# Expert rows fetched by index against all expert tiles streamed through the matrix engine

## The chip, the cores and the metric

The kernel runs on one core of a Trainium2 chip. The engines of a core are TensorE (PE in the profile, its weight loads PEld), VectorE (DVE), ScalarE (ACT), GpSimd (POOL) and SyncE (SP, which only issues transfers here). The metric is the device time of one execution in microseconds (us), lower is better. The program is one launch, all in float32.

## The reference

A first block of two layers (convolution, attention, cross-attention, layer norm) is followed by a second one: attention and a gated recurrence, merged and added to x, then an expert layer, then a gated projection of side inputs. The change touches the expert layer, cut here to its core:

```python
def peer_ffn(h, w_q, sub_keys, u, v):          # T = 512 tokens, D = 1024, 8 heads, K = 16 picks a head
    q = (ht @ w_q).reshape(T, PEER_HEADS, 2, PEER_DKEY // 2)
    s = jnp.einsum('thpc,hpnc->thpn', q, sub_keys)
    v1, i1 = lax.top_k(s[:, :, 0], K)
    v2, i2 = lax.top_k(s[:, :, 1], K)
    cand = (v1[..., :, None] + v2[..., None, :]).reshape(T, PEER_HEADS, K * K)
    cand_idx = (i1[..., :, None] * PEER_NKEYS + i2[..., None, :]).reshape(T, PEER_HEADS, K * K)
    top_s, pos = lax.top_k(cand, K)
    idx = jnp.take_along_axis(cand_idx, pos, axis=-1)
    g = jax.nn.softmax(top_s, axis=-1)
    # per block of 128 tokens:
    ue = jnp.take(u, ib, axis=0)               # u, v: 16384 x 1024, float32, 64 MiB each
    w = jax.nn.gelu(jnp.einsum('thkd,td->thk', ue, xb)) * gb
    out = jnp.einsum('thk,thkd->td', w, jnp.take(v, ib, axis=0))
```

Each token so needs 128 of the 16384 rows of u and as many of v.

## The kernel before

Tokens lie 128 to a block, four blocks. Everything up to the merged sum of the second block is a chain of matrix products over 2 MB weight slots, which SP streams into two buffers W (L505) as PE gives them back (`used`, L547); the change leaves it alone. Around position 1700 us of the span the part begins that is changed:

- PE runs `xT_f(0)`, `xT_f(1)` (transposes of the normed rows of blocks 0 and 1), `queries` for one of the four slots of w_q, `merge(2)` and `merge(3)` (the last products of blocks 2 and 3, L988), and then the remaining queries. `queries` is `project_fm` (L537, 32 products of 128x256 or 128x512) and then the products with the sub-keys (L1034); ACT copies the results out (L1490, L1137) and counts up `sk_ready`.
- DVE selects the picks, one head of one block at a time (`route_step`, L2116 to L2153): the 16 best of two lists of 128 scores, the 256 sums of these pairs, the 16 best sums, and the two ranks turned back into key numbers by comparing with 0 to 15 (L2144 to L2147).
- As soon as a head has its picks, POOL issues one indexed transfer for each of its 16 picks (`gather_u`, L1567): 128 rows of u, one for each token, 512 KB, into a ring of 8. DVE multiplies and sums each against h (L2246), ACT and DVE make gelu and softmax of 16 numbers a token, and POOL fetches the same picks' rows of v (L1583). ACT writes a diagonal matrix of the 128 weights (L1446) and PE multiplies it with the rows of v, two products of 128x512 (L1017), summed in a bank for each block and half. There are 512 transfers of u and 512 of v; 10 of the last ones are added by DVE.
- Each block that is complete runs its last step (`ple_*`, L1079 to L1106, L2211) beside the picks of the others; the last block's is the end of the program.

The order on each engine is fixed in the program; nothing is scheduled at run time but by semaphores.

## Time and profile before

| | us |
|---|---|
| median of 3 runs (3283.68 to 3296.66) | 3289.33 |
| span of the profiled execution, first to last instruction | 3278.9 |
| PE busy / DVE / ACT / POOL in it | 2812.3 / 1829.2 / 652.2 / 1273.9 |
| read from HBM | 662.19 MB |

The profile is of one execution; its page gives the span and no separate time, so the span stands for it, and the timed median lies 10.4 us above it. "x n" counts instructions; each float32 product shows as two records, a transpose as one. The granted clock of PE is given as a share of its full level of 2.4 GHz.

### The profile page before, as it was taken

How to read it: one execution, taken by the hardware profiler on the slowest of the kernel's cores; microseconds unless marked ns; L12 is line 12 of the kernel's file. 1: busy time of each engine (PE TensorE's matmuls, PEld its weight loads, DVE VectorE, ACT ScalarE, POOL GpSimd, SP SyncE). 2: the span in 40 equal slices, each digit the busy share in tenths (PEclk: the TensorE clock that was granted, in tenths of full speed). 3: DMA queues.
4: the chain of work that ended last, by engine and by line, in shares of the span. 5: the costliest groups of instructions: out<-in, count | busy, mean ns of one | idle time of the engine just before them, and what ended most of it. 6: DMA issues, size and time to landing. Idle time of an engine off the chain costs nothing.

```text
span 3278.9 us, 26326 instructions
## 1 busy us (share of the span) xinstructions
PE 2812.3 (86%) x7932; PEld 1338.4 (41%) x7932; DVE 1829.2 (56%) x4230; ACT 652.2 (20%) x1556; POOL 1273.9 (39%) x1113
## 2 busy tenths in 40 slices
PE   9999999998889899988898889777768786777778
PEld 4455445454554444555555334322223232222323
DVE  4989502058751322267529666576666666666643
ACT  1114301022320112344401111111111111111111
POOL 0520000000000000022104767777777777777774
PEclk9999999999999999999999999999989999999999
DMA  4221122220112111001216999999999999999996
GB/s 179 77 103 52 64 77 77 77 77 26 51 40 77 67 69 51 26 30 49 90 65 216 366 371 368 371 387 373 345 361 371 363 353 367 372 366 352 368 386 244
DMA packets 161469, 665.89 MB, mean 203 GB/s; under 512 B 17856, under 2 KB 18240, under 8 KB 154304
## 3 DMA queue, kind: packets, MB, share of 16 engines
q0 software_dynamic: 147456, 536.94, 43.9%
q1 hardware_dynamic: 12032, 117.43, 9.8%
q10 hardware_dynamic: 1856, 10.00, 0.8%
q8 instruction: 61, 1.00, 0.1%
q14 instruction: 64, 0.52, 0.0%
HBM read 662.19 MB, written 2.10 MB: 203 GB/s over the span
## 4 chain that ended last, share of the span: by engine, by line
PE 54%; POOL 18%; issue 9%; DVE 9%; DMA 7%; ACT 2%; another core or an unknown queue 0%; DVEq 0%; ACTq 0%; POOLq 0%; SPq 0%
PE ps L537 13%; PE ps L1017 8%; POOL G L1567 8%; PE ps L652 6%; POOL H L1583 5%; POOL XT L1583 4%; PE ps L589 4%; PE ps L882 3%; DMA XT<-peer_v,C 3%; DMA H<-peer_v,C 3%; PE ps L790 2%; PE ps L911 2%; PE ps L819 2%; DMA G<-peer_u,C 2%; PE ps L976 2%
## 5 line engine op out<-in xcount | busy, mean ns | idle before, releaser
L2246 DVE CUSTOM_DVE_ANT_0 G<-G,H 128x1024 f32<-128x1024 f32 x512 | 627.7, 1226 | 465.7 <-DMA G<-peer_u,C 396.0
L1017 PE MATMUL ps<-H,MK 128*128 128x512 f32 x1196 | 591.2, 623 | 190.3 <-DMA H<-peer_v,C 124.0
L1567 POOL DMA_INDIRECT G<-peer_u,C x512 | 540.3, 1055 | 302.9 <-issue 151.8
L537 PE MATMUL ps<-XT,W 128*128 128x512 f32 (+1 forms) x1344 | 543.0, 553 | 8.9 <-issue 6.5
L1017 PE MATMUL ps<-XT,MK 128*128 128x512 f32 x812 | 403.1, 629 | 130.6 <-DMA XT<-peer_v,C 80.3
L1017 PEld LDWEIGHTS ps<-H,MK 128*128 128x128 f32 x1196 | 218.6, 195 | 532.3 <-issue 476.0
L1583 POOL DMA_INDIRECT H<-peer_v,C x304 | 350.6, 1153 | 131.3 <-issue 71.8
L537 PEld LDWEIGHTS ps<-XT,W 128*128 128x128 f32 x1344 | 254.1, 190 | 294.2 <-issue 286.2
L1017 PEld LDWEIGHTS ps<-XT,MK 128*128 128x128 f32 x812 | 149.5, 197 | 381.1 <-issue 326.0
L1542 POOL COPY PR<-H 128x256 f32<-128x256 f32 x4 | 1.4, 392 | 781.2 <-DVE H L1871 781.2
L1446 ACT ACTIVATE MK<-C 128x128 f32<-128x128 f32 x502 | 175.0, 393 | 524.5 <-PE ps L1017 292.6
L1583 POOL DMA_INDIRECT XT<-peer_v,C x208 | 241.1, 1159 | 78.7 <-issue 48.5
L652 PE MATMUL ps<-W,Y 128*128 128x512 f32 x512 | 226.1, 603 | 13.1 <-DVE Y L1746 6.1
L589 PE MATMUL ps<-XT,W 128*128 128x512 f32 x448 | 220.5, 604 | 1.6 <-ACT G L1152 1.6
L1554 POOL TENSOR_TENSOR H<-H 128x256 f32<-128x256 f32 x56 | 47.6, 852 | 353.9 <-ACT H L1376 320.6
L1645 DVE SCALAR_TENSOR_TENSOR Y<-H,V,Y x240 | 165.3, 765 | 0.0
L652 PEld LDWEIGHTS ps<-W,Y 128*128 128x128 f32 x512 | 98.3, 193 | 140.3 <-issue 137.1
L1433 ACT ACTIVATE H<-C 128x16 f32<-128x16 f32 x32 | 6.9, 216 | 630.3 <-DVE H L2162 336.8
L1528 POOL TENSOR_TENSOR H<-H,SIG 128x512 f32 x12 | 73.5, 6125 | 111.9 <-ACT SIG L1212 108.9
L1755 DVE SCALAR_TENSOR_TENSOR X<-X,H 128x512 f32<-128x512 f32 x16 | 11.1, 691 | 181.9 <-ACT H L1137 181.9
L589 PEld LDWEIGHTS ps<-XT,W 128*128 128x128 f32 x448 | 80.6, 195 | 59.7 <-issue 55.7
L882 PE MATMUL ps<-W,XT 128*128 128x512 f32 x192 | 98.5, 622 | 0.3 <-issue 0.3
(296 smaller groups left out, 3121.3 us busy)
## 6 DMA issues: line engine op xcount, KB each, us to landing
W<-wstream SPq DMA_DIRECT2D x51, 2048.0 KB
G<-peer_u,C POOLq DMA_INDIRECT x512
H<-peer_v,C POOLq DMA_INDIRECT x304
XT<-peer_v,C POOLq DMA_INDIRECT x208
XT<-xT SPq DMA_DIRECT2D x8, 256.0 KB, 5.3
W<-wstream SPq DMA_DIRECT2D x8, 256.0 KB, 5.8
X<-x SPq DMA_DIRECT2D x1, 2048.0 KB, 19.0
SIG<-rows ACTq DMA_DIRECT2D x4, 512.0 KB, 6.4
```

The lines of the kernel that those rows point to most:

```text
L537: mm = pe.matmul(b[:, 0:rhs[k].shape[-1]], w[:, k, m * P:(m + 1) * P], rhs[k], start=(k == 0), stop=(k == KD - 1))
L589: mm = pe.matmul(FILL_BANK[j % 2][:, :], w[:, k, m * P:(m + 1) * P], XT[:, k, :], start=(k == 0), stop=(k == KD - 1))
L652: mm = pe.matmul(ps[pos % 4][:, :], Y[:, (j * KD + k) * T + b * P:(j * KD + k) * T + (b + 1) * P], w[:, k, :], start=(j == 0 and k == 0), ...
L790: mm = pe.matmul(ps[p0 % 4][:, 0:n], XT[:, k, b * P:(b + 1) * P], w[:, k, 0:n], start=(k == 0), stop=(k == KD - 1))
L882: mm = pe.matmul(ring(pos)[:, :], XT[:, k, b * P:(b + 1) * P], w[:, k, :], start=(k == 0), stop=(k == KD - 1))
L1017: mm = pe.matmul(ps[2 * b + half][:, :], DG[by_tensor(v - 1) % DIAG_RING], VB[at][:, half * T:(half + 1) * T], start=(n == FIRST[b] and k ...
L1446: act.activation(DG[at % DIAG_RING], ident, ACT.Copy, scale=GW[:, v:v + 1]).then_inc(diag_full, 1)
L1528: pool.tensor_tensor(hrow(i * 4 + j, TAPS - 1, T), hrow(i * 4 + j, TAPS - 1, T), SIG[:, j, :], ALU.mult).then_inc(glu_done, 1)
L1567: pool.indirect_dma_start(UB[u % U_RING], None, peer_u, bass.IndirectOffsetOnAxis(ap=IDX[:, u:u + 1], axis=0)).then_inc(u_loaded[u % U_RIN ...
L1583: pool.indirect_dma_start(VB[at], None, peer_v, bass.IndirectOffsetOnAxis(ap=IDX[:, v:v + 1], axis=0)).then_inc(v_loaded[at], 16)
L1645: ins = dve.scalar_tensor_tensor(yt(c), hrow(c, k, T), V[:, ds(c * TAPS + (FM["conv_w"] + k), 1)], yt(c), ALU.mult, ALU.add)
L2246: dve.tensor_tensor_reduce(out=rows_u, in0=rows_u, in1=tm(H, 0, D, group(n)[0]), scale=1.0, scalar=0.0, op0=ALU.mult, op1=ALU.add, accum_o ...
```

## The change

The expert layer no longer fetches rows by index. All 128 tiles of 128 experts are streamed in order, u and v of a tile side by side in 1 MB, and every expert is computed for every token; a gate that is zero for an expert that was not picked takes the rest out. The sums for 256 tokens take four of the eight PSUM banks, so the whole is done twice: blocks 0 and 1 in steps 0 to 127, blocks 2 and 3 in steps 128 to 255.

- A step on PE: `expert_dots` (8 products of 128x256, tile of u as weights), then `expert_sums` of the step before (4 products of 128x512, the gated activations as weights, tile of v moving). ACT takes gelu of the 128x256, DVE multiplies with the gates (`weigh`).
- The gates: the picks (two key numbers and the softmax weight, 128 a token) are transposed; for each token one matrix 128x128 with a one in each column's first key, one with the weight at the second key, and their product is that token's 128x128 table of gates. For blocks 0 and 1 this stands ahead of step 0 (64 groups of 4 tokens), for blocks 2 and 3 it lies in steps 37 to 127 (128 pairs of tokens), and DVE selects their picks in steps 0 to 80.
- The queries are computed for blocks 0 and 1 first and for 2 and 3 later, so w_q is loaded twice. The norm ahead of them moves to ACT in part, with its gain put in when the transposes are copied out.
- Selection handles two heads at once (`route`, 35 instructions and more for each of 16 units); the softmax is made over a whole block.
- Buffers are placed by hand over one another (ARENA). The scores of blocks 2 and 3 wait in DRAM.
- POOL has no work left in this part. The last step of blocks 0 and 1 lies in steps 212 to 243, that of 2 and 3 behind step 255.

```diff
-GROUPS = NB * PEER_HEADS
-PICKS = GROUPS * PEER_K
-U_RING = 8
-V_RING = 8
-DIAG_RING = 8
-V_BEHIND = 24
-V_EARLY = 96
-V_LATE = PICKS - 30
-DIAG_AHEAD = 6
-A_RING = 8
-GELU_C = float(np.sqrt(2 / np.pi))
+TILES = 128
+ARENA = 217504
+STEPS = 2 * TILES
+UV_RING = 3
+WA_RING = 4
+PICKED_2, PICKED_3 = 33, 82
...
-                ("gate_c", 4), ("up", 2), ("wq", 4), ("ple", 2)])
+                ("gate_c", 4), ("up", 2), ("wq", 8), ("ple", 2)])
...
+            sp.wait_ge(bank_full, POS["wq3b"] + 6)
+            for m in range(STEPS + 1):
+                if m == UV_RING:
+                    sp.wait_ge(a_full, 1)
+                elif m > UV_RING:
+                    sp.wait_ge(w_used, m - UV_RING)
+                sp.dma_start(UV[:, m % UV_RING, :], experts[m % TILES]).then_inc(uv_loaded[m % UV_RING], 16)
...
-            def expert_row(v):
...
+            for q in range(4):
+                queries(f"wq{q}a", q, (0, 1))
             merge(2)
             merge(3)
...
             xT_f(3)
+            for q in range(4):
+                queries(f"wq{q}b", q, (2, 3))
+
+            def expert_dots(g):
+
+                at = g % UV_RING
+                u = UV[:, at, 0:D].rearrange("p (k e) -> p k e", k=KD)
+                pe.wait_ge(uv_loaded[at], 16 * (g // UV_RING + 1))
+                if g >= 2:
+                    pe.wait_ge(gelu_done, g - 1)
+                c0 = (g // TILES) * 256
+                for k in range(KD):
+                    mm = pe.matmul(UP_BANK[g % 2][:, 0:256], u[:, k, :], XT[:, k, c0:c0 + 256],
+                                   start=(k == 0), stop=(k == KD - 1))
...
+            def expert_sums(g):
+
+                at, j = (g + 1) % UV_RING, g % TILES
+                pe.wait_ge(w_ready, g + 1)
...
+                        mm = pe.matmul(acc(b, n)[:, :], WA[:, g % WA_RING, b * P:(b + 1) * P],
+                                       UV[:, at, D + n * T:D + (n + 1) * T], start=(j == 0), stop=(j == TILES - 1),
+                                       skip_group_check=True)
...
+            def build_pair(p):
+
+                pe.wait_ge(pair_hot, 2 * p + 2)
+                pe.wait_ge(pair_one, p + 1)
+                if p >= 2:
+                    pe.wait_ge(gates_kept, p - 1)
+                for i in range(2):
+                    mm = pe.matmul(BUILD_BANK[p % 2][:, i * P:(i + 1) * P], OHB[:, (2 * p + i) % 6, :], OHB[:, 6 + (2 * p + i) % 6, :],
+                                   start=True, stop=True)
+                mm.then_inc(built, 1)
...
+            pe.wait_ge(tail_free, made)
+            expert_dots(0)
+            for b in range(2):
+                bank(POS["it"] + b)
+                picks_transposed(ring(POS["it"] + b), b).then_inc(bank_full, 1)
+            for n in range(64):
+                pos = POS["build"] + n
+                bank(pos)
+                pe.wait_ge(hot, 4 * n + 4)
+                pe.wait_ge(ones_made if n < 32 else ones_b, n % 32 + 1)
+                for i in range(4):
+                    one = GATES_0[:, 128 + 4 * n + i, :] if n < 32 else ONES_KEPT[:, n % 4, i, :]
+                    mm = pe.matmul(ring(pos)[:, i * P:(i + 1) * P], OHB[:, (4 * n + i) % 12, :], one, start=True, stop=True)
+                mm.then_inc(bank_full, 1)
...
+            for g in range(STEPS):
+                if g + 1 < STEPS:
+                    expert_dots(g + 1)
+                for b in (2, 3):
+                    if g == (PICKED_2, PICKED_3)[b - 2] + 1:
+                        if b == 3:
+                            pe.wait_ge(gates_kept, pairs_by(g - 1))
+                        picks_transposed(MISC_BANK, b).then_inc(it_full, 1)
+                        pe.wait_ge(it_copied, b - 1)
+                for p in pairs_of(g):
...
+                expert_sums(g)
+            ple_transposes(2)
+            ple_transposes(3)
+            for b in (2, 3):
+                ple_gates(b, 0)
+                ple_gates(b, 1)
+                ple_proj(b)
...
+            def gelu(g):
+
+                act.wait_ge(a_full, g + 1)
+                if g >= WA_RING:
+                    act.wait_ge(w_used, g - WA_RING + 1)
+                act.activation(WA[:, g % WA_RING, :], UP_BANK[g % 2][:, 0:256], ACT.Gelu_apprx_tanh).then_inc(gelu_done, 1)
+
+            def pair_ones(p):
+
+                if p % 64 == 0:
+                    act.wait_ge(it_copied, p // 64 + 1)
+                if p >= 3:
+                    act.wait_ge(built, p - 2)
+                at = 6 + (2 * p) % 6
+                for i in range(2):
+                    n = ac.count(act.activation(OHB[:, at + i, :], IOTA, ACT.Abs, scale=-1.0,
+                                                bias=IT[:, 0, 2 * p + i:2 * p + i + 1]))
+                ac.after(n)
+                act.activation(OHB[:, at:at + 2, :], OHB[:, at:at + 2, :], ACT.Relu, scale=-1.0, bias=1.0
+                               ).then_inc(pair_one, 1)
+
+            def keep_pair(p):
+
+                act.wait_ge(built, p + 1)
+                act.wait_ge(w_ready, p + 1)
+                act.activation(GATES_1[:, :, :, p], BUILD_BANK[p % 2][:, 0:256].rearrange("p (q i) -> p q i", q=2), ACT.Copy
...
+            exponentials(0)
+            drain(POS["it"], lambda bk: act.activation(
+                IT[:, :, 0:P], bk[:, 0:3 * P].rearrange("p (i t) -> p i t", i=3), ACT.Copy))
+            act.wait_ge(bank_free, POS["it"] + 1 + 4)
+            act.wait_ge(scores_out, 32)
+            for n in range(32):
+                for i in range(4):
+                    last = ac.count(act.activation(GATES_0[:, 128 + 4 * n + i, :], IOTA, ACT.Abs, scale=-1.0,
+                                                   bias=IT[:, 0, 4 * n + i:4 * n + i + 1]))
+                ac.after(last)
+                act.activation(GATES_0[:, 128 + 4 * n:132 + 4 * n, :], GATES_0[:, 128 + 4 * n:132 + 4 * n, :], ACT.Relu,
+                               scale=-1.0, bias=1.0).then_inc(ones_made, 1)
+            exponentials(1)
+            drain(POS["it"] + 1, lambda bk: act.activation(
+                IT[:, :, P:2 * P], bk[:, 0:3 * P].rearrange("p (i t) -> p i t", i=3), ACT.Copy))
+            gelu(0)
+            for n in range(64):
+                drain(POS["build"] + n, copy_to(GD[:, n * T:(n + 1) * T]))
+            act.wait_ge(bank_free, POS["end"] + 4)
+            act.dma_start(KEPT[:, :], kept[0]).then_inc(scores_back, 16)
...
+            for g in range(STEPS):
+                for b in (2, 3):
+                    if g == (PICKED_2, PICKED_3)[b - 2] + 1:
+                        picks_copied(b)
+                for p in pairs_of(g + 1):
+                    pair_ones(p)
+                if g + 1 < STEPS:
+                    gelu(g + 1)
+                for p in pairs_of(g):
+                    keep_pair(p)
...
-            def gather_u(u):
...
-            def gather_v(v):
...
+            drawn(route(0, 0))
+            drawn(route(0, 1))
+            unit = route(0, 2)
+            drawn(unit, 16)
+            residual_sum(2)
+            drawn(unit)
+            row_factor(2)
+            residual_sum(3)
+            unit = route(0, 3)
+            drawn(unit, 16)
+            row_factor(3)
+            drawn(unit)
+            soft_start(0)
+            unit = route(1, 0)
+            drawn(unit, 12)
+            soft_end(0)
+            drawn(unit)
+            for q in range(1, 4):
+                drawn(route(1, q))
+            soft_start(1)
+            soft_end(1)
+
+            def hot_row(at, t, done):
+                dve.tensor_scalar(OHB[:, at, :], IOTA, IT[:, 1, t:t + 1], IT[:, 2, t:t + 1], ALU.is_equal, ALU.mult
+                                  ).then_inc(done, 1)
+
+            rows4 = [P, 4, P]
...
+            for n in range(64):
+                if n % 32 == 0:
+                    dve.wait_ge(bank_free, POS["it"] + n // 32 + 1 + 4)
+                if n >= 3:
+                    dve.wait_ge(bank_full, POS["build"] + n - 2)
+                for i in range(4):
+                    hot_row((4 * n + i) % 12, 4 * n + i, hot)
+                if n >= 32:
+                    if n >= 36:
+                        dve.wait_ge(bank_full, POS["build"] + n - 3)
+                    dve.tensor_tensor(ONES_KEPT[:, n % 4, :, :],
+                                      IOTA.rearrange("p (t i) -> p t i", t=1).broadcast_to(rows4),
+                                      IT[:, 0, 4 * n:4 * n + 4].rearrange("p (t i) -> p t i", i=1).broadcast_to(rows4),
+                                      ALU.is_equal).then_inc(ones_b, 1)
+
+            def weigh(g):
+
+                if g == 0:
+                    dve.wait_ge(bank_free, POS["end"] + 4)
+                if g == TILES:
+                    dve.wait_ge(gates_kept, TILES)
+                dve.wait_ge(gelu_done, g + 1)
+                w = WA[:, g % WA_RING, :]
+                if g < TILES:
+                    dve.tensor_tensor(w, w, GATES_0[:, :, g], ALU.mult).then_inc(w_ready, 1)
+                else:
+                    w = w.rearrange("p (j q) -> p q j", q=2)
+                    dve.tensor_tensor(w, w, GATES_1[:, :, g - TILES, :], ALU.mult).then_inc(w_ready, 1)
+
+            def hot_pair(p):
...
+            for g in range(STEPS):
+                weigh(g)
+                for p in pairs_of(g + 1):
+                    hot_pair(p)
+                if g < PICKED_3 - 1:
+                    i, quota = route_quota(g)
+                    drawn_of[i] += drawn(routes[i], quota - drawn_of[i])
...
```

ACT, from the last queries to the first work for the experts. Before (EXPS and the diagonals stand behind the third of the half queries):

```order
L1426 ACTIVATE XT<-ps 128x4x128 [waits bank_full] x3
L1490 ACTIVATE SIG<-ps 128x256 [waits bank_full] x4
L1137 ACTIVATE Y<-ps 128x512 [waits bank_full] x2
L1433 ACT_TABLE_LOAD [waits bank_free]
L1433 ACTIVATE H<-C 128x16 [waits tanh_in]
L1434 ACTIVATE H<-H 128x16
L1446 ACTIVATE MK<-C 128x128 [waits weights]
L1446 ACTIVATE MK<-C 128x128 x6
```

And now, behind the eighth query (EXB holds the exponents of the softmax, IT the transposed picks, GD the gates):

```order
L1513 ACTIVATE SIG<-ps 128x256 [waits bank_full] x3
L1195 ACTIVATE Y<-ps 128x512 [waits bank_full] x2
L1522 ACT_TABLE_LOAD [waits bank_free]
L1522 ACTIVATE EXB<-EXB 128x128 [waits soft_in]
L1601 ACTIVATE IT<-ps 128x3x128 [waits bank_full]
L1607 ACTIVATE GD<-C,IT 128x128 [waits scores_out,bank_free]
L1607 ACTIVATE GD<-C,IT 128x128 x3
```

The first exponential now stands behind all query copies of all four blocks, and the one-hot rows L1607 behind it.

DVE at the same place of the changed program (L2268 starts the softmax of block 0, L2272 ends it, L2212 to L2221 are the selection of block 1, L2309 the rows that hold the weights); there is no softmax of a block before, but a head's:

```order
L2268 TENSOR_TENSOR EXB<-BG 128x128 [waits dve_link]
L2212 MAX TOPV<-KEPT 128x8 [waits sk_ready]
L2212 MAX TOPV<-KEPT 128x8 x3
L2216 MAX_INDEX TOPI<-TOPV,KEPT 128x8 [waits dve_link] x4
L2221 MATCH_REPLACE KEPT<-TOPV,KEPT 128x128 [waits dve_link] x4
L2272 TENSOR_REDUCE SMX<-EXB 128x8 [waits soft_exp]
L2273 RECIPROCAL SMX<-SMX 128x8 [waits dve_link]
L2274 TENSOR_TENSOR BG<-EXB,SMX 128x128 [waits dve_link]
L2212 MAX TOPV<-KEPT 128x8 [waits dve_link]
```

```order
L2259 TENSOR_REDUCE PK<-HOT 128x2x32 [waits dve_link]
L2268 TENSOR_TENSOR EXB<-BG 128x128 [waits dve_link]
L2272 TENSOR_REDUCE SMX<-EXB 128x8 [waits soft_exp]
L2273 RECIPROCAL SMX<-SMX 128x8 [waits dve_link]
L2274 TENSOR_TENSOR BG<-EXB,SMX 128x128 [waits dve_link]
L2309 TENSOR_SCALAR OHB<-C,IT 128x128 [waits bank_free]
L2309 TENSOR_SCALAR OHB<-C,IT 128x128 x11
L2309 TENSOR_SCALAR OHB<-C,IT 128x128 [waits bank_full]
```

The wait for `soft_exp` stands in the middle of the selection of block 1, and the first L2309 behind the whole of it.

PE in the stage of the experts, before (a diagonal as weights, rows of v moving):

```order
L1017 MATMUL ps<-XT,MK 128x512 [waits v_loaded4,diag_full]
L1017 MATMUL ps<-XT,MK 128x512
L1017 MATMUL ps<-XT,MK 128x512 [waits v_loaded5,diag_full]
L1017 MATMUL ps<-XT,MK 128x512
...
L1017 MATMUL ps<-H,MK 128x512 [waits v_loaded0,diag_full]
L1017 MATMUL ps<-H,MK 128x512
```

And a step with a pair of tokens now:

```order
L1072 MATMUL ps<-UV,WA 128x512 [waits w_ready]
L1072 MATMUL ps<-UV,WA 128x512 x3
L1056 MATMUL ps<-XT,UV 128x256 [waits gelu_done,uv_loaded2]
L1056 MATMUL ps<-XT,UV 128x256 x7
L1095 MATMUL ps<-OHB 128x128 [waits pair_one,pair_hot]
L1095 MATMUL ps<-OHB 128x128
L1072 MATMUL ps<-UV,WA 128x512 [waits w_ready]
L1072 MATMUL ps<-UV,WA 128x512 x3
```

Waits for a fetched row and a diagonal at each pair of products become one wait for the tile and one for the gated activations in a step of 12 products.

## Rows read from the trace of the kernel before

**Rows 1.** The page: chain of waits by engine, DVE's dots, PE's diagonal products.
```profile
PE 54%; POOL 18%; issue 9%; DVE 9%; DMA 7%; ACT 2%; another core or an unknown queue 0%; DVEq 0%; ACTq 0%; POOLq 0%; SPq 0%
L2246 DVE CUSTOM_DVE_ANT_0 G<-G,H 128x1024 f32<-128x1024 f32 x512 | 627.7, 1226 | 465.7 <-DMA G<-peer_u,C 396.0
```

**Rows 2.** Windows: us, busy of PE, PEld, DVE, ACT, POOL, clock, DMA, GB/s.
```profile
1200.00:1300.00 100.00, 99.45 (x306) 46.35 (x305) 15.56 (x46) 23.13 (x47) 0.00 (x0) 1.00 0.18 66
1789.00:3279.00 1490.00, 1135.06 (x2472) 450.83 (x2472) 934.29 (x2368) 225.53 (x664) 1102.14 (x999) 0.96 0.96 360
```

**Rows 3.** Timeline of PE: start, us, instructions, idle before.
```profile
1702.12 1.94 PE L575 MATMUL ps<-C,H 128*128 128x128 f32 x16 [0.26 <-issue]
1719.47 2.05 PE L1034 MATMUL ps<-MK,SIG 128*128 128x128 f32 x16 [0.47 <-ACT SIG L1490]
1721.36 1.04 PE L575 MATMUL ps<-C,MK 128*128 128x128 f32 x8
...
1730.38 7.03 PE L988 MATMUL ps<-H,XT 128*128 128x512 f32 x16
1737.25 1.04 PE L575 MATMUL ps<-C,MK 128*128 128x128 f32 x8
...
1772.28 14.05 PE L537 MATMUL ps<-XT,W 128*128 128x256 f32 x64 [1.17 <-issue]
...
1789.12 0.67 PE L537 MATMUL ps<-XT,W 128*128 128x256 f32 x2 [0.26 <-issue]
1801.08 3.66 PE L1017 MATMUL ps<-H,MK 128*128 128x512 f32 x4 [11.29 <-DMA H<-peer_v,C]
...
1805.01 1.88 PE L1017 MATMUL ps<-H,MK 128*128 128x512 f32 x4
```

**Rows 4.** Timeline of ACT in the same stretch.
```profile
1712.13 0.38 ACT L1490 ACTIVATE SIG<-ps 128x256 f32<-128x256 f32 x1 [3.07 <-PE ps L537]
1715.58 0.38 ACT L1490 ACTIVATE SIG<-ps 128x256 f32<-128x256 f32 x1 [3.07 <-PE ps L537]
...
1788.00 0.60 ACT L1137 ACTIVATE Y<-ps 128x512 f32<-128x512 f32 x1 [1.25 <-PE ps L1034]
1789.60 1.28 ACT L1433 ACT_TABLE_LOAD   x1
...
1794.08 2.15 ACT L1446 ACTIVATE MK<-C 128x128 f32<-128x128 f32 x7 [2.77 <-DVE C L2171]
```

**Rows 5.** Timeline of DVE: two heads selected one after the other, then block 2's sum.
```profile
1722.24 0.62 DVE L2116 MAX8 H<-Y 128x8 f32<-128x128 f32 x2 [18.86 <-ACTq L1494]
...
1733.17 0.62 DVE L2116 MAX8 H<-Y 128x8 f32<-128x128 f32 x2
...
1744.28 1.29 DVE L2075 TENSOR_TENSOR X<-X,ps 128x512 f32<-128x512 f32 x2
```

**Rows 6.** Groups of DVE by form, from 1600 us: busy, mean ns.
```profile
L2144 DVE TENSOR_TENSOR H<-H,C 128x256 f32<-128x256 f32 x64 | 26.9, 421 | 0.1
...
L2138 DVE TENSOR_SCALAR H<-H 128x16 uint32<-128x16 uint32 x32 | 5.5, 171 | 0.1
...
L2193 DVE TENSOR_SCALAR Y<-ps,V 128x128 f32<-128x128 f32 x16 | 4.5, 345 | 0.9 <-PE ps L1079 0.8
```

**Rows 7.** DMA issues: KB each, median us to landing.
```profile
X<-x SPq DMA_DIRECT2D x1, 2048.0 KB, 19.0
...
Y<-wstream ACTq DMA_DIRECT2D x1, 2048.0 KB, 8.1
...
MK<-subkeys ACTq DMA_DIRECT2D x1, 1024.0 KB, 5.6
```

**Rows 8.** Timeline of all engines at the end.
```profile
3253.76 3.67 PE L1017 MATMUL ps<-XT,MK 128*128 128x512 f32 x8 [1.08 <-DMA XT<-peer_v,C]
...
3260.26 13.97 PE L1091 MATMUL ps<-W,Y 128*128 128x512 f32 x32 [0.72 <-ACT Y L1455]
```

736 lines of the change are left out of this document (360 added, 376 removed), and 5 rows, old and new, of the table at.

## The prediction

> **What bounds the kernel now.** I read the chain of waits first, then the groups of instructions, then windows and timelines. The chain names PE for 54%, then POOL, DVE and DMA in pieces [rows 1]: up to 1700 us the program is a row of matrix products, and the last 1490 us are something else. In the first part PE is busy 99% of a window at a granted clock of 1.00 [rows 2]. In the stage of the experts PE is busy 1135 of 1490 us, while the transfers hold 0.96 of the DMA engines at 360 GB/s, and DVE's dots wait 396 us for rows of u [rows 1, 2]. So this stage is set by the bytes it fetches: 1024 transfers of 512 KB are 537 MB, and at 360 GB/s that is 1491 us. It starts near 1789 and ends with the span. This is what the change can take away, and it replaces it by 2 x 128 tiles of 1 MB = 268 MB, half the bytes, and by far more products.
>
> **What a step costs on PE.** The price of float32 products stands in the trace twice. With 256 columns: ACT copies out a bank each time 8 of them are done, and two copies start 3.45 us apart [rows 4]; that is 0.431 us a product. With 512 columns: 16 records (8 products) from 1730.38 to the next group at 1737.25 are 6.87 us, 0.859 a product [rows 3]. A step has 8 of the first and 4 of the second: 3.45 + 3.44 = 6.89 us. 256 steps are 1764; the first dots stand ahead of the loop, so 1760. Nothing can hide this, PE is the engine that works, and it alone is longer than the stage that it replaces (1490).
>
> Also on PE in the loop: the 128 pairs of the second half, 256 products of 128 columns at 0.236 (16 records from 1719.47 to 1721.36 [rows 3]) = 60 us; the last step of blocks 0 and 1, 40 products of 512 columns = 34, and 16 transposes at 0.12 [rows 3] = 2; twice a wait until ACT has copied the transposed picks, 2 each = 4. Loop: 1760 + 60 + 36 + 4 = 1860. The waits at tile and gated activations cost nothing if they are met early: products of two kinds with waits between them follow at full pace from 1805 on [rows 3]. If each step lost 0.1 at a wait it would be 26 more.
>
> Here a rule of the Trainium skill speaks against the change, and the rows first: in the window 1200 to 1300 PE is busy 99.45 us and the weight loads 46.35 us more, 146 us in 100, so loads run beside products [rows 2], with 256 columns too, where 64 records take 14.05 us [rows 3]. The page "TensorE: Matmul & The Clock Gate" of the Trainium skill, section "Part 3: Packing small matmuls — row/col tiling", says that a weight load overlaps products in flight only when it goes to another row group. Every product here uses all rows, so by the rule each of 24 loads a step would add to it; that is rival four below.
>
> **Ahead of the loop.** Positions in the span:
> - Transposes of blocks 0 and 1 start at 1702.1 as before. Their copies now carry the gain in pieces of 128x128, 16 at the 0.29 of ACT's seven in a row (2.15 less one's 0.39, by 6 [rows 4]) = 4.7: queries from 1707.
> - A query of two blocks is 16.84, from 1772.28 to 1789.12 [rows 3]. Four stand ahead of the merges now: 1774.5. The second load of w_q is hidden, a 2 MB slot landed in 8.1 [rows 7] and a query takes twice that; SP's queue then holds the scores' way out (2 MB) ahead of the first tiles, which have until 1955.
> - Two merges, 15.9 each (1721.36 to 1737.25 [rows 3]): 1806.3. They come 53 us later than before, and block 3's sum on DVE, which sits in the middle of block 0's selection, waits for them. Then the sum 0.65 (half of 1.29 for two [rows 5]), square and root on ACT 1.4, 16 selection instructions 5.5 (a quarter of the 22.04 for two heads [rows 5]), scaling 1.2 (DVE's 1024 elements are 1.23 [rows 1]), transposes and copies 2.5, 11 us: queries of blocks 2 and 3 from 1817, and again 67.4: 1884.5.
> - ACT's first exponential stands behind the last of these copies: table load 1.28 [rows 4] and itself, 1886. DVE has finished block 0 and 12 instructions of block 1 at about 1830 and waits 56 us for it, with the rest of block 1's selection queued behind.
> - One `route` (two heads): before, two heads one after the other are 22.04 us [rows 5]. Of that, 12 instructions of 256 elements become 3 of 1024 (0.42 against 1.23 [rows 1, 6], each with 0.03 to the next: 12 x 0.45 against 3 x 1.26): -1.7; the 14 short ones of 0.17 [rows 6] and their gaps become 5: -2; fewer links and one sum of 512 instead of two: -0.9. 17.4. DVE still owes 13 of the started one and three more: 1886 + 13 + 52 = 1951, softmax, transposes and copy 4: 1955. ACT's one-hot rows run beside it (32 x about 1.9 = 61 from 1894, when the scores are out in DRAM): also 1955. If these rows take 0.39 each without overlap it is 1970.
> - The 64 groups of the first half: PE needs 4 x 0.236 = 0.95, ACT a copy of 0.60 [rows 4]; DVE 4 rows of 128x128 with two scalars, which the trace doesn't show. Bounds: 0.17 (16 elements) and 0.345 (128 from PSUM, [rows 6]); I take 0.26. 32 groups at 1.05, and 32 at 1.7, since the comparison for 4 tokens (128x512, half of the 1.29 for two [rows 5]) joins: 88 us, with bounds of 74 and 110. Loop starts at 1955 + 88 + 2 = 2045.
>
> On these rows the Trainium skill's page "VectorE: DVE Perf Modes", section "What auto-detection actually checks", says that an operation with one source in SBUF takes two float32 elements a cycle. By its 0.96 GHz a row would be 0.07 shorter than one from PSUM; an estimate by that page makes the groups some 6 us shorter than I take them. No row here shows this size.
>
> **Behind it.** From the last products (3253.76 + 3.67) to the end of the span are 21.5 us with one block's gate products of 13.97 in it [rows 8]. Now two blocks stand there and the side products are not done earlier: 21.5 + 13.7 + 2 x 3.4 = 42.
>
> Sum: 2045 + 1860 + 42 = 3947 against a span of 3278.9; with the 10.4 around it 3957.
>
> **What lies beside.** DVE in a step: 0.42 for the gates, in steps 0 to 31 four to five selection instructions (70 us in 32 steps, 2.2 each), later 1.5 and up to four rows at 0.26: under 4 of 6.89. The gates are read 512 bytes apart; from 0.42 (packed, [rows 6]) to four times that it stays hidden, because gelu and gates have a whole step to be ready: `expert_sums` of step g waits behind the sums of g-1 and the dots of g+1. ACT: 0.4 for gelu, two pairs at 1.5: 3.4. Transfers: 1 MB took 5.6 us and 2 MB 8.1 [rows 7]; each has 13.8 us from the buffer's release to its use and two are under way.
>
> **The rivals.**
> 1. Gates or gelu late: a row of long selection instructions (three of 1.26) or a slow strided read passes 6.89 - 0.4 - 0.4 = 6 us in a step, from there each us counts. For: all three engines meet at every step. Against: 4 us as worked out. 1 us in each of the first 128 steps: 3957 + 128 = 4085.
> 2. The stream is late: the slowest 2 MB took 19.0 [rows 7], 9.5 a tile, 2.6 over the step: 256 x 2.6 = 670, 4627. That one was issued among other transfers at the start; the stage now moves 360 GB/s and needs 152.
> 3. Not slower: the stage goes at the pace of its bytes, as it does now. 268 MB at 360 GB/s are 746 us, and 2045 + 746 + 42 + 10 = 2843. It decides below (3279 - 2045 - 42 - 100) / 256 = 4.27 us a step. For: DMA is what this stage waits for today. Against: the products of a step are priced by rows at full clock, 6.89; they would have to be 38% cheaper than anywhere in this trace.
> 4. Weight loads not hidden: 46.35 / 305 = 0.15 each [rows 2], 24 a step: 3.6 x 256 = 930, 4890. The same window contradicts it. It is the skill's rule above; the trace disagrees with it.
> 5. The clock. After 11.29 us of waiting four records took 3.66 instead of 1.88 [rows 3], the lower of the two levels. That is paid once or twice ahead of the loop (PE waits from 1890 to 1955), 2 to 5 us; in the loop PE has no waits that would bring it. Inside the forecast's range.
>
> **Chances.** The forecast 0.86, its own range 3910 to 4040 (groups -14 to +22, ACT's rows to +15, waits in the loop 0 to +26, slips ahead of the loop +20). Rival 1 0.06, rival 2 0.03, rival 3 0.03, rival 4 0.01; 0.01 that the result is level for a cause that I don't see. A measurement of this kernel can tell about 0.5% from no change. So slower 0.96, same 0.01, faster 0.03. The range, 3900 to 4070, leaves out the top of rival 1 and all others.
>
> **What would show it.** Step: 256 dots groups 6.9 us apart where no pair lies between, 7.4 to 7.8 with pairs, PE over 98% busy at clock 1.00 from 2045 on. DVE idle some 56 us ahead of L2272 once, and the loop's first L1072 at 2045 to 2050. HBM read about 400 MB, DMA near 0.4 in the loop. Wrong if PE waits for `w_ready` or the tiles over 50 us in sum, if products of 256 columns are not half those of 512, or if the groups of the first half take over 110 us.

## The result, and the profile after

The changed kernel takes 3945.72 us (median of 4 runs, 3944.23 to 3946.36); the kernel before took 3286.51 beside it (3272.77 to 3296.66). The ratio is 1.2018 [1.1991, 1.2044]: 20% slower, against 3957 us forecast.

The page of the changed kernel: span, busy time, the chain of waits by engine, groups of instructions, the tiles' transfers.

```profile
span 3942.3 us, 35590 instructions
PE 3727.5 (95%) x13232; PEld 2284.9 (58%) x13232; DVE 1357.3 (34%) x3436; ACT 876.1 (22%) x2011; POOL 142.7 (4%) x89
...
HBM read 404.83 MB, written 4.19 MB: 104 GB/s over the span
...
PE 88%; DVE 7%; ACT 3%; issue 2%; DMA 0%; DVEq 0%; POOL 0%; ACTq 0%; SPq 0%; POOLq 0%
...
L1056 PE MATMUL ps<-XT,UV 128*128 128x256 f32 x4096 | 928.0, 380 | 11.0 <-DMA UV<-experts 10.8
L1072 PE MATMUL ps<-UV,WA 128*128 128x512 f32 x2048 | 920.8, 592 | 0.6 <-ACT IT L1555 0.6
...
L2340 DVE TENSOR_TENSOR WA<-WA,GD 128x256 f32<-128x256 f32 x128 | 54.6, 426 | 850.3 <-ACT WA L1529 850.3
...
L2337 DVE TENSOR_TENSOR WA<-WA,GD 128x256 f32<-128x256 f32 x128 | 77.6, 606 | 625.3 <-ACT WA L1529 623.4
...
UV<-experts SPq DMA_DIRECT2D x257, 1024.0 KB, 4.8
```

PE's share of the chain went from 54% to 88%. POOL (18% before [rows 1]) and DMA (7%) are gone from it, and DVE went from 9% to 7%. The bytes fell from 662 to 405 MB. PE waited for a tile once (10.8 us, at the first dots, ahead of the loop). For the gated activations it never waited: the 0.6 us at L1072 is a wait for ACT's copy of the transposed picks. DVE and ACT do the waiting now. The multiplication with the gates took 0.606 us where 256 gates lie 512 bytes apart (blocks 0 and 1), and 0.426 where they lie packed in two runs of 128, with the activations read and written at a step of two words (blocks 2 and 3).

Windows of the changed kernel (columns as in [rows 2]), ahead of the loop and inside it:

```profile
1885.00:1960.00 75.00, 7.80 (x26) 6.23 (x27) 54.60 (x212) 59.32 (x164) 0.00 (x0) 0.55 0.19 69
1960.00:2050.00 90.00, 74.02 (x529) 66.42 (x528) 83.72 (x281) 39.76 (x67) 0.00 (x0) 0.98 0.03 12
2050.00:2300.00 250.00, 249.42 (x870) 164.85 (x869) 81.80 (x287) 19.07 (x46) 0.00 (x0) 1.00 0.46 156
3000.00:3500.00 500.00, 500.00 (x1747) 331.65 (x1746) 30.67 (x72) 27.65 (x72) 0.00 (x0) 1.00 0.48 165
```

From 3000 to 3500 PE is busy for every one of 500 us at clock 1.00, while the transfers hold 0.48 of the DMA engines. The stage of [rows 2], which moved 360 GB/s at a share of 0.96, has become one that moves 165 at the pace of its products.

The timeline of PE in the changed kernel (columns as in [rows 3]): the start of the queries for blocks 2 and 3, their end, the hole ahead of the gates, the start of the loop, a step with a pair, the end.

```profile
1813.45 15.87 PE L534 MATMUL ps<-XT,W 128*128 128x256 f32 x64 [2.21 <-issue]
...
1878.82 2.05 PE L1015 MATMUL ps<-MK,SIG 128*128 128x128 f32 x16 [0.47 <-ACT SIG L1513]
1891.65 5.67 PE L1056 MATMUL ps<-XT,UV 128*128 128x256 f32 x16 [10.78 <-DMA UV<-experts]
1897.15 0.38 PE L1085 MATMUL ps<-C,PK 128*128 128x128 f32 x2
...
1958.08 0.66 PE L1085 MATMUL ps<-C,PK 128*128 128x128 f32 x2 [60.44 <-DVE BG L2274]
...
1959.07 11.16 PE L1149 MATMUL ps<-GD,OHB 128*128 128x128 f32 x75
...
2045.31 3.62 PE L1056 MATMUL ps<-XT,UV 128*128 128x256 f32 x16
2048.77 3.60 PE L1072 MATMUL ps<-UV,WA 128*128 128x512 f32 x8
2052.20 3.62 PE L1056 MATMUL ps<-XT,UV 128*128 128x256 f32 x16
...
2679.74 0.61 PE L1095 MATMUL ps<-OHB 128*128 128x128 f32 x4
2680.18 3.60 PE L1072 MATMUL ps<-UV,WA 128*128 128x512 f32 x8
2683.62 3.62 PE L1056 MATMUL ps<-XT,UV 128*128 128x256 f32 x16
2687.07 0.61 PE L1095 MATMUL ps<-OHB 128*128 128x128 f32 x4
...
3894.09 7.03 PE L1072 MATMUL ps<-UV,WA 128*128 128x512 f32 x16
...
3903.74 13.97 PE L1122 MATMUL ps<-GD 128*128 128x512 f32 x32 [0.39 <-issue]
```

A step is 2052.20 - 2045.31 = 6.89 us, with a pair 2687.07 - 2679.74 = 7.33. The loop goes from 2045.31 to 3901.12: 1855.8. The tail behind it is 41.2. So the 663 us that the span grew by (3942.3 - 3278.9) have three parts: the loop starts 256 us behind 1789, near which the stage of the experts started before; it is 366 us longer than the 1490 us of that stage; and the tail, which lay inside the 1490, is another 41.

DVE and then ACT in the changed kernel, the same stretch: three holes of the one, one of the other ahead of the gates.

```profile
1883.25 0.29 DVE L2272 TENSOR_REDUCE SMX<-EXB 128x8 f32<-128x128 f32 x1 [61.66 <-ACT EXB L1522]
...
1898.28 0.75 DVE L2212 MAX8 BG<-CAND 128x8 f32<-128x256 f32 x2 [11.39 <-ACT IT L1601]
...
1957.08 0.29 DVE L2272 TENSOR_REDUCE SMX<-EXB 128x8 f32<-128x128 f32 x1 [7.36 <-ACT EXB L1522]
```

```profile
1897.68 0.49 ACT L1601 ACTIVATE IT<-ps 128x384 f32<-128x384 f32 x1 [14.46 <-PE ps L1085]
1898.21 1.28 ACT L1607 ACTIVATE GD<-C,IT 128x128 f32<-128x128 f32 x4
1899.52 0.63 ACT L1610 ACTIVATE GD<-GD 128x512 f32<-128x512 f32 x1
1900.05 1.26 ACT L1607 ACTIVATE GD<-C,IT 128x128 f32<-128x128 f32 x4
```

DVE's first hole is the wait for the exponential behind the queries' copies, as forecast. The second was not forecast: block 1's best sums go into BG, which holds block 0's weights until they are transposed, and those transposes stand on PE behind the first dots, which wait for tile 0. ACT waits for the same transposes, 14.5 us, and then makes its 32 groups of one-hot rows, one each 1.83 us, 58.6 in sum: 1898.2 to 1956.8. Block 1's exponential stands behind them; that is DVE's third hole. So of the two chains that lead to the gates, one over DVE's selection and one over ACT's one-hot rows, ACT's ended last.

### The profile page after: what moved, and what is told of

Read it like the earlier page. It is cut to its first block, busy times and chain, and to the rows that moved or that the text cites. A ratio compares the mean times of both kernels' runs of the same rounds, so it can differ in the third digit from the quotient of the medians.

```text
span 3942.3 us, 35590 instructions
## 1 busy us (share of the span) xinstructions
PE 3727.5 (95%) x13232; PEld 2284.9 (58%) x13232; DVE 1357.3 (34%) x3436; ACT 876.1 (22%) x2011; POOL 142.7 (4%) x89
## 4 chain that ended last, share of the span: by engine, by line
PE 88%; DVE 7%; ACT 3%; issue 2%; DMA 0%; DVEq 0%; POOL 0%; ACTq 0%; SPq 0%; POOLq 0%
PE ps L1056 22%; PE ps L1072 22%; PE ps L534 13%; PE ps L649 5%; PE ps L586 3%; PE ps L879 2%; PE ps L787 2%; PE ps L908 2%; PE ps L816 2%; DVE OHB L2309 2%; PE ps L1095 1%; PE ps L985 1%; PE ps L973 1%; PE ps L1122 1%; ACT GD L1607 1%
## 5 line engine op out<-in xcount | busy, mean ns | idle before, releaser
L1056 PE MATMUL ps<-XT,UV 128*128 128x256 f32 x4096 | 928.0, 380 | 11.0 <-DMA UV<-experts 10.8
L1072 PE MATMUL ps<-UV,WA 128*128 128x512 f32 x2048 | 920.8, 592 | 0.6 <-ACT IT L1555 0.6
L1056 PEld LDWEIGHTS ps<-XT,UV 128*128 128x128 f32 x4096 | 779.4, 190 | 226.2 <-issue 133.0
L1072 PEld LDWEIGHTS ps<-UV,WA 128*128 128x128 f32 x2048 | 382.0, 190 | 379.6 <-issue 370.7
L1529 ACT ACTIVATE WA<-ps 128x256 f32<-128x256 f32 x256 | 98.2, 384 | 1485.9 <-PE ps L1056 1485.9
L2340 DVE TENSOR_TENSOR WA<-WA,GD 128x256 f32<-128x256 f32 x128 | 54.6, 426 | 850.3 <-ACT WA L1529 850.3
L2337 DVE TENSOR_TENSOR WA<-WA,GD 128x256 f32<-128x256 f32 x128 | 77.6, 606 | 625.3 <-ACT WA L1529 623.4
L2309 DVE TENSOR_SCALAR OHB<-C,IT 128x128 f32<-128x128 f32 x512 | 142.5, 342 | 32.3 <-PE ps L1095 31.2
L1539 ACT ACTIVATE OHB<-C,IT 128x128 f32<-128x128 f32 x256 | 84.8, 381 | 29.1 <-PE ps L1095 29.1
L1765 DVE SCALAR_TENSOR_TENSOR Y<-H,V,Y 128x512 f32<-128x512 f32 x120 | 81.1, 745 | 0.0
L1095 PEld LDWEIGHTS ps<-OHB 128*128 128x128 f32 x512 | 71.2, 191 | 5.4 <-ACT IT L1555 0.8
```

The costliest lines, as they stand in the source:

```text
L1056: mm = pe.matmul(UP_BANK[g % 2][:, 0:256], u[:, k, :], XT[:, k, c0:c0 + 256], start=(k == 0), stop=(k == KD - 1))
L1072: mm = pe.matmul(acc(b, n)[:, :], WA[:, g % WA_RING, b * P:(b + 1) * P], UV[:, at, D + n * T:D + (n + 1) * T], start=(j == 0), stop=(j == ...
L1095: mm = pe.matmul(BUILD_BANK[p % 2][:, i * P:(i + 1) * P], OHB[:, (2 * p + i) % 6, :], OHB[:, 6 + (2 * p + i) % 6, :], start=True, stop=True)
L1529: act.activation(WA[:, g % WA_RING, :], UP_BANK[g % 2][:, 0:256], ACT.Gelu_apprx_tanh).then_inc(gelu_done, 1)
L1539: n = ac.count(act.activation(OHB[:, at + i, :], IOTA, ACT.Abs, scale=-1.0, bias=IT[:, 0, 2 * p + i:2 * p + i + 1]))
L2309: dve.tensor_scalar(OHB[:, at, :], IOTA, IT[:, 1, t:t + 1], IT[:, 2, t:t + 1], ALU.is_equal, ALU.mult).then_inc(done, 1)
```

## The experiments

The experiments ran on three chips: the first four on one, the next four on a second and the last three on a third. The kernel before was timed beside each group: 3283.14, 3292.22 and 3227.46 us. A ratio is always to the time of its own group; times and spans of kernels whose loop is set by PE are compared with the changed kernel's directly (two edits that should change nothing, below, came within 1.4 us of it).

The theory: the time is PE's float32 products, 6.89 us a step, and nothing else in the loop counts; ahead of the loop a chain over DVE and ACT sets the start. The rivals: the step is set by the tiles' transfers, by ACT and DVE between dots and sums, or by a fixed cost of each step.

**Half of the sums.** In the steps in between, the sums for the second 512 columns are left out.

```
+                        if n == 1 and 0 < j < TILES - 1:
+                            continue
                         mm = pe.matmul(acc(b, n)[:, :], ...
```

> Leaves out the second 512 output columns of the weighted sums in tiles 1 to 126 of both passes: 504 of the 1024 products of 128x512; everything else, the 1 MB a step too, stays. Theory (the loop runs at PE's price of the columns, 0.859 us a product): 504 x 0.859 = 433 us less, 3946 -> 3513. Rival (the stream sets the step): no change, 3946. Rival (gelu and gates arrive just in time, the step is their chain): under 100 us less, with PE waiting for w_ready.

3514.83 us (3514.51 to 3517.16), ratio 1.0697 [1.0665, 1.0729], span 3513.0: 429.3 us less than the changed kernel's span. Left out are 2 x 126 steps of two products: 252 x 2 x 0.859 = 433. So nearly every us of products taken out is a us of time.

**Half of the dots too.** Four of the eight dots (k 2 to 5) left out as well.

```
+                    if 1 < k < 6:
+                        continue
```

> As half_sums, and 4 of the 8 dots of each step left out too: 1024 products of 128x256 at 0.431 are another 441 us. Theory: a step of 3.45 us, 3946 - 433 - 441 = 3072, since the stream then needs 305 GB/s and the engines beside PE at most 4 us in some steps (selection, up to 30 us late in sum): 3070 to 3110. Rival stream: if 1 MB can't come faster than every 4.8 us (its time to landing), 256 x 4.8 = 1229 for the loop, 3300. Rival chain: 3500 or more.

3085.83 us (3084.72 to 3086.63), ratio 0.9389 [0.9361, 0.9417], span 3083.8. Again 429 less (255 x 4 x 0.431 = 440 are left out). A step is down to 2 x 1.72 = 3.44 us, half of 6.89, below the 4.27 at which the third rival was to decide, and the kernel is faster than before. The transfers still keep up: where no pairs lie between the steps they move 305 GB/s, and PE is busy all the time.

```profile
2600.00:2700.00 100.00, 100.00 (x350) 66.25 (x349) 12.37 (x29) 11.14 (x29) 0.00 (x0) 1.00 0.85 305
```

**A fifth of a step.** Two dots and one product of the sums.

```
+                    if 0 < k < 7:
+                        continue
...
+                        if b + n > 0 and 0 < j < TILES - 1:
+                            continue
```

> Leaves out 6 of 8 dots a step, and 3 of 4 weighted sums in tiles 1 to 126: PE needs 1.72 us a step. Theory: PE alone would give 2635; the next bound is the stream, 268 MB at the 360 GB/s that the gathers reached, 2.9 us a step, so 2850 to 3000, with PE waiting for tiles by then. If a tile can't follow before 2 x its time to landing in a ring of three (4.8 / 2 = 2.4 a step) that is hidden behind it. A rival in which DVE or ACT bound the first 128 steps (selection, rows, gates, 3 to 4 us a step): 3000 to 3150, with PE's waits on w_ready.

2934.33 us (2922.96 to 2939.84), ratio 0.8919 [0.8884, 0.8955]. Only 148 us less in the span (2935.4), though about as many us of products are gone again. Two windows of this run, a piece of the loop and the whole loop:

```profile
2500.00:2700.00 200.00, 136.49 (x368) 74.36 (x367) 26.00 (x61) 23.43 (x61) 0.00 (x0) 0.89 0.94 351
2043.00:2894.00 851.00, 637.19 (x2170) 374.19 (x2168) 320.74 (x993) 305.36 (x802) 0.00 (x0) 0.94 0.87 323
```

In the first window PE is busy 136 of 200 us and the transfers hold 0.94 at 351 GB/s: now the tiles set the pace, and PE waits 195 us for them in the loop. The time is 91 us over the third rival's 2843, the floor of the bytes. The second window shows where they are: over the whole loop the stream makes 323 GB/s at a share of 0.87, and the loop takes 851 us, where 746 were worked out from 360 GB/s (105 more; the loop's start, the tail and the times around the span give 11 back in this execution, which took 2937.34). PE waits only 14 us for gated activations, so DVE's work accounts for little of it.

**The upper halves.** The lower 16 bits of each operand of dots and sums are not used: a float32 word's upper half, read with a step of two, is the number as bf16. Count, columns and order of the products stay.

```
+def high(a, n):
+    return a.bitcast(BF16).rearrange("p (n two) -> p n two", two=2)[:, 0:n, 1]
...
-  mm = pe.matmul(UP_BANK[g % 2][:, 0:256], u[:, k, :], XT[:, k, c0:c0 + 256],
+  mm = pe.matmul(UP_BANK[g % 2][:, 0:256], high(u[:, k, :], P), high(XT[:, k, c0:c0 + 256], 256),
...
-  mm = pe.matmul(acc(b, n)[:, :], WA[...], UV[...], ...
+  mm = pe.matmul(acc(b, n)[:, :], high(WA[...], P), high(UV[...], T), ...
```

> No product is left out, but the dots and the weighted sums read only the upper 16 bits of each float32 word (as bfloat16, every second 16-bit element): same bytes streamed, same instructions, one pass for each product instead of four. Theory (PE's price is four passes a column at 0.42 ns): 8 x 0.11 + 4 x 0.215 = 1.74 us a step, as in fifth_step, so the same time as fifth_step within 2%, 2850 to 3150. Rival (the price is the read of 4-byte elements or of the weights, not the passes): weight loads at 0.19 are 24 or 12 a step and PE stays at 3.5 to 6.9, 3070 to 3946. Operands are cut to 8 bits of mantissa, the picks are not.

2911.11 us (2902.85 to 2916.77), ratio 0.8861 [0.8827, 0.8895]. PE's timeline and the window in this run:

```profile
2131.44 1.08 PE L1063 MATMUL ps<-XT,UV 128*128 128x256 bf16 x8 [2.25 <-DMA UV<-experts]
2132.36 1.06 PE L1079 MATMUL ps<-UV,WA 128*128 128x512 bf16 x4
2133.85 1.08 PE L1063 MATMUL ps<-XT,UV 128*128 128x256 bf16 x8 [0.42 <-DMA UV<-experts]
```

```profile
2500.00:2700.00 200.00, 139.43 (x771) 74.41 (x772) 27.27 (x64) 24.58 (x64) 0.00 (x0) 0.91 0.95 364
```

Eight dots are 0.92 us instead of 3.45 (2131.44 to 2132.36). With every product in its place, only cheaper, the same change is a gain: what costs is the price of float32 products, not their number or the steps' waits. Now PE waits for tiles, which come at 364 GB/s in this window. (The kernel computes with less precise operands; whether that is enough is for its user to judge.)

**The exponential earlier.** Ahead of the loop: ACT takes block 0's exponential behind the first of the late queries' copies.

```
             for q in range(4):
                 queries(f"wq{q}b", q, (2, 3))
+                if q == 0:
+                    exponentials(0)
 
-            exponentials(0)
```

> ACT's first exponential stands behind the first query of blocks 2 and 3 instead of behind the last: soft_exp comes near 1831 instead of 1883. Forecast's picture (DVE waits 54 us for it with block 1's selection behind): the first row of L2309 about 50 us earlier if nothing else is late. Theory after reading the trace: the selection of block 1 is stopped again 3 us later by its write over BG, which waits until PE has transposed block 0's picks; PE does that behind all queries and behind the first dots, which wait for the first tile until 1891.6 (ACT's copy at 1898.2). So 0 to 1 us, 3944 to 3946, and DVE idle ahead of L2212 on BG 60 us instead of 11.

3944.34 us (3943.38 to 3946.23), ratio 1.1974 [1.1941, 1.2006]: nothing. DVE in this run:

```profile
1833.80 0.29 DVE L2273 TENSOR_REDUCE SMX<-EXB 128x8 f32<-128x128 f32 x1 [12.64 <-ACT EXB L1522]
...
1898.14 0.75 DVE L2213 MAX8 BG<-CAND 128x8 f32<-128x256 f32 x2 [60.71 <-ACT IT L1602]
```

The hole of 61.7 us shrank to 12.6, and the second one, 11.4, grew to 60.7. The wait for BG ends at 1898 as before, and with it ACT's wait for the same transposes.

**The transposes ahead of the dots.** Block 0's picks are transposed before the first dots.

```
-            expert_dots(0)
             for b in range(2):
                 bank(POS["it"] + b)
                 picks_transposed(ring(POS["it"] + b), b).then_inc(bank_full, 1)
+                if b == 0:
+                    expert_dots(0)
```

> PE transposes block 0's picks ahead of the first dots instead of behind them. Theory: copy at 1885 instead of 1898; DVE's selection of block 1 goes on 11 us earlier, ACT's one-hot rows start when the scores are out (about 1889), 9 us earlier; the first group of the gates at 1949 instead of 1958: 3946 - 9 = 3937. Rival (the exponential sets this part): no change.

3935.77 us (3935.05 to 3936.52), ratio 1.1947 [1.1914, 1.1979]; span 3933.1, 9.2 less. PE in this run:

```profile
1884.66 0.41 PE L1085 MATMUL ps<-C,PK 128*128 128x128 f32 x2 [3.38 <-DVE BG L2275]
...
1950.33 9.91 PE L1150 MATMUL ps<-GD,OHB 128*128 128x128 f32 x69
```

The gates start at 1950.33 instead of 1959.07. ACT in this run begins its rows so much earlier:

```profile
1889.48 1.28 ACT L1608 ACTIVATE GD<-C,IT 128x128 f32<-128x128 f32 x4 [3.77 <-DMA scores_kept<-Y]
```

That is 8.7 us before 1898.21, and it is now the scores' way out to DRAM that they wait for. So the place of the transposes cost 9 us, by way of ACT's rows.

**More work for DVE in each step of the second half.** Three, and in another kernel six, operations over 1024 elements ahead of the gates.

```
             for g in range(STEPS):
+                if TILES <= g < STEPS - 1:
+                    for _ in range(6):
+                        ch.link(dve.tensor_tensor(HOT[:, :], HOT[:, :], HOT[:, :], ALU.max))
                 weigh(g)
```

> Three operations of 128x1024 on DVE (3.8 us) are put ahead of each step's gates in steps 128 to 254, result unused. Theory: PE sets the step and the gates have 6.88 - 0.38 - 0.43 = 6.0 us of slack: no change, 3946, DVE 4.2 us busy a step. Rival (the chain gelu, gates is what the step waits for, or DVE's reads slow PE's): up to 127 x 3.8 = 480 more.

3944.62 us (3943.96 to 3947.09), ratio 1.1972 [1.194, 1.2005]: nothing, with 3.8 us more on DVE in each of 127 steps.

> Six such operations, 7.6 us with their links, and 0.43 for the gates, so 8.0 a step on DVE alone, over the 6.88 of PE. Theory: above the point DVE sets the step: 127 x (8.0 - 6.9) = 140 more, 4085, and PE waits for w_ready about 1.1 a step. If the point lay lower (no overlap of the chain across steps), it would be 127 x (0.4 + 8.0) = 1070 or more in place of 875, over 4140.

4048.64 us (4048.36 to 4049.72), ratio 1.229 [1.2257, 1.2323]. DVE and PE in this run:

```profile
3303.80 7.52 DVE L2385 TENSOR_TENSOR HOT<-HOT 128x1024 f32<-128x1024 f32 x6
3311.35 0.43 DVE L2340 TENSOR_TENSOR WA<-WA,GD 128x256 f32<-128x256 f32 x1
```

```profile
3303.94 3.70 PE L1072 MATMUL ps<-UV,WA 128*128 128x512 f32 x8 [0.74 <-DVE WA L2340]
...
3311.83 3.70 PE L1072 MATMUL ps<-UV,WA 128*128 128x512 f32 x8 [0.74 <-DVE WA L2340]
```

And its waits (what waits for what: us in total, times, the longest), from 2950 us on:

```profile
PE ps L1072 <- DVE WA L2340: 76.0, 101, 1.8
```

A step is 7.89 us now on both engines, and on DVE it holds nothing but its own work: 3303.45 to 3311.35, six operations and the gates. Gelu does not add to it, since the operations run beside it. So the point of the first rival lies at 6.5 us of other work, not at 6, and past it each us counts (6.89 less the 0.43 of the gates; no run lies between 3.8 and 7.5 us of added work). The sum is +103 us, not 140: PE waits in 101 of the 127 steps, 101 x 1.0 = 101. In the others the 36 us of products of the last steps of blocks 0 and 1 keep PE longer than DVE.

**The whole way to the loop.** Both edits above, with second buffers for the picks of block 1, and the one-hot rows interleaved: ACT makes those of 7 groups ahead and then those of every second group beside the products, DVE the rest (32 groups each, as before, and not the 36 and 28 of the expectation), instead of 32 groups of ACT's ahead of everything. ACT's rows now lie in eight slots, clear of the scores, so its wait for their way out to DRAM moves behind the rows and the first gelu. Dots and sums in float32.

```
+ACT_ONES = list(range(7)) + list(range(7, 56, 2))
+DVE_ONES = [n for n in range(64) if n not in ACT_ONES]
...
+        PKS, BGS = (PK, PK1, PK, PK), (BG, BG1, BG, BG)
...
             for n in range(64):
                 drain(POS["build"] + n, copy_to(GD[:, n * T:(n + 1) * T]))
+                if n + 6 in ACT_ONES[7:]:
+                    ones_of(ACT_ONES.index(n + 6))
```

> The part ahead of the loop without its three waits, products as in the changed kernel: exponential behind the first query of blocks 2 and 3; own copies of picks for block 1, so that its selection need not wait for the transposes; transposes ahead of the first dots; one-hot rows made by ACT and DVE by turns, 36 and 28 groups. Theory: selection of block 1 ends near 1897, first group of the gates near 1900 instead of 1958, the 64 groups 84 to 90 us: loop at 1987 instead of 2045, 3946 - 58 = 3888. Rival (another wait, the first tile or the scores' way out, takes over): 3925 or more.

3886.48 us (3884.15 to 3886.68), ratio 1.2043 [1.1962, 1.2123] against 3227.46 (3210.05 to 3255.02), the time of the kernel before beside these last three. The ratio is no better than the 1.2018 above because the kernel before is 59 us faster here, so the gain is read from the spans. The loop in this run:

```profile
1985.33 3.62 PE L1061 MATMUL ps<-XT,UV 128*128 128x256 f32 x16
1988.79 3.60 PE L1077 MATMUL ps<-UV,WA 128*128 128x512 f32 x8
```

It starts 60.0 us earlier (2045.31), and the span is 60.0 shorter (3942.3 to 3882.3). A us ahead of the loop is a us of time, but these 60 are a tenth of what the change costs (3945.72 - 3286.51 = 659).

**The same with the upper halves.** This edit and `high` together.

> lead_in and high_halves together. Theory: the two gains lie in different parts and add: 2911 - 58 = 2853, 13% under the kernel before. Rival: a loop that is set by the stream gains less, since in the present one the ring is full at its start either way: 2853 to 2880.

2845.24 us (2842.02 to 2863.92), ratio 0.8836 [0.8769, 0.8902], span 2840.1: the fastest version, ahead of both kernels, if 16 bits of each operand may go. By its ratio it can't be told from the upper halves alone (0.8861), since it is compared with a faster kernel before. Its trace shows the gain: the dots ahead of the first sums start at 1985.97 instead of 2043.93, 58.0 earlier, and that is most of the 63.3 us between the two spans.

**The upper halves in the kernel before.** To see whether bf16 products alone would do: the products with the diagonals (L1017) read upper halves, nothing else is changed.

```
-  mm = pe.matmul(ps[2 * b + half][:, :], DG[...], VB[at][:, half * T:(half + 1) * T],
+  mm = pe.matmul(ps[2 * b + half][:, :], high(DG[...], P), high(VB[at][:, half * T:(half + 1) * T], T),
```

> The kernel before (rows fetched by index) with its 502 pairs of products of diagonal and rows of v on the upper 16 bits of each word, so 0.215 instead of 0.859 a product: PE has 1004 x 0.64 = 646 us less work in a stage of 1490. Theory: this stage is set by its 537 MB, so 0 to 1% less, 3250 to 3290. Rival (the chain of waits names PE for most of it): 100 us less or more.

3213.11 us (3199.84 to 3227.11), ratio 0.9948 [0.9916, 0.9979] against the kernel before. Window of this run, to be read against the second line of [rows 2]:

```profile
1789.00:3279.00 1490.00, 636.30 (x1440) 175.87 (x1466) 933.57 (x2365) 217.69 (x663) 1083.63 (x998) 0.62 0.94 360
```

PE works 499 us less, at a granted clock of 0.62 instead of 0.96, and the transfers still hold 0.94 of the DMA engines (the window's last 62 us lie behind the span's end, so the rate within the stage is above the 360 GB/s that it shows; from 2500 to 2700 it is 382, against 365 in the kernel before on its own chip). The 3250 to 3290 us of the expectation were counted from the time on the other chip; against 3227.46 the time is 0.5% less, within its 0 to 1%: the stage was set by its bytes, as the prediction read it. So the gain of the upper halves comes only together with half the bytes.

## Why the prediction was right

- **A step**, 6.89 us from two spacings of the kernel before [rows 3, 4]: measured 6.89. The experiments on dots and sums show that it is the sum of its products, down to half of them.
- **The loop**, 1860: measured 1855.8. A pair costs 7.33 - 6.89 = 0.44 and not 0.47, 128 pairs 56 instead of 60; 255 dots groups of 3.45 and 256 sums of 3.436 are 1759.4 of it.
- **The waits** at tile and gated activations: 0 to 26 us were left open, and there are none. DVE waits for gelu in both halves, 623.4 us in the first and 850.3 in the second, 4.9 and 6.6 a step. The first rival's point (6 us) was half a us too low by what six more operations cost, since gelu lies beside DVE's other work.
- **Ahead of the loop**: the queries of blocks 2 and 3 start at 1813.45, not 1817; DVE, ready sooner, waits 61.7 us and not 56. DVE's selection needs from 1883.8 to 1949.7, less the 11.4 in between, 54.5 us where 65 were forecast; ACT's rows end at 1956.8 where 1955 was forecast for both. That both ends came out near 1955 is in part luck: DVE's was 10.5 us too large in its work and lacked the wait of 11.4, and ACT's rows began 4 us later than forecast and took 2.5 less. The groups take 2045.31 - 1959.07 = 86 against 88.
- **What was missed**: "the first tiles, which have until 1955". They did not have so long, because the first dots stand ahead of the transposes of block 0's picks, and ACT's rows and the second use of BG behind these. Tile 0 was there at 1891, PE waited 10.8, ACT 14.5, DVE 11.4. The early queries made up for part of it; transposes first gave 9 us.
- **DVE's rows of 128x128**, where two bounds stood for a missing row, 0.17 and 0.345, and a rule of the Trainium skill's "VectorE: DVE Perf Modes", section "What auto-detection actually checks", stood beside them. Measured:

```profile
2040.86 1.12 DVE L2309 TENSOR_SCALAR OHB<-C,IT 128x128 f32<-128x128 f32 x4
```

Four are 1.12 us and the page of the profile has 0.342 for one, so they start (1.12 - 0.34) / 3 = 0.26 apart, the value taken. The length is that of the operation from PSUM, 0.345 [rows 6], but that does not speak against two elements a cycle. The trace of the kernel before has float32 operations with one source in SBUF in its earlier layers, one of them of this very size, which the prediction called missing:

```profile
L1710 DVE TENSOR_SCALAR SIG<-SIG,RI 128x128 f32<-128x128 f32 x12 | 3.4, 287 | 0.4
L1710 DVE TENSOR_SCALAR SIG<-SIG,RI 128x512 f32<-128x512 f32 x12 | 5.8, 487 | 0.4
```

384 elements more take 0.200 us more, 0.52 ns each. That is two a cycle at the 0.96 GHz that this page of the Trainium skill gives, so the trace agrees with that rule. With two scalars from SBUF, as in the new rows, 1024 elements take 0.812 us (L1720 of the changed kernel) and 128 take 0.342: again 0.52 ns an element. At 1024 elements the operation with one scalar takes 0.754 (L1935 there), so the second costs 0.06, and 0.287 + 0.06 is the 0.342 measured. The 6 us that the prediction derives from the rule are not worked out there and do not follow from 0.07 a row; its sum does not use them.
- **The tail**, 42: measured 41.2, with 13.97 for the gate products as before [rows 8].
- **The 10.4 around the span** is a term of the sum that was wrong in kind. The execution of 3942.3 us of span was timed at 3944.23. What surrounds a span is 2 us. With these the profiled execution of the kernel before took some 3281 us, less than any of its three timed runs (3283.68 to 3296.66); the rest of the 10.4 is this spread. The span was 4.7 us off, this term 7.
- **Weight loads beside products**: PE and PEld sum to 832 us in a window of 500 (3000 to 3500), so they overlap; and if a load of 0.19 us stood in the time of a product, one of 256 columns (0.431) could not cost half of one of 512 (0.859). The rule of "TensorE: Matmul & The Clock Gate" of the Trainium skill, section "Part 3: Packing small matmuls — row/col tiling", by which loads overlap only in another row group, doesn't hold for these products of 128 rows. The same section also says that a load to the background weight buffer is pulled ahead of products in flight; that would allow the overlap seen here, but no run shows which buffer a load goes to.
- **The clock** fell only in the hole ahead of the gates (0.55 from 1885 to 1960) and was back at 0.98 in the next window, as the fifth rival had it.

Left open: why the stream of tiles makes 323 GB/s over the loop of the run with a fifth of a step, and not 360, which is the 91 us over the floor of the bytes (2843). A load is issued only when PE has given back a buffer of three; no run has a longer ring.

## What to carry to other kernels

Trading bytes for products pays only up to a point that can be worked out beforehand: a stage that waits for its transfers at 360 GB/s is worth its bytes over that rate, and what replaces it is worth its products at the spacing that the same trace shows, here 1490 against 1855 us. What has to be ready before the new stage can start counts too: here it was 256 us, against 366 for the loop. If it stands on the wrong side of the point (4.27 us a step here, 6.89 needed), look at the price of one product before anything else: waits, order and the way to the loop were worth 60 us together, the format of the operands 1035 (3945.72 - 2911.11). And a hole that an edit closes can reappear at the next wait of the same engine (61.7 and 11.4 us became 12.6 and 60.7): before counting a hole as gain, look for the chain that ends last.
